# First layer of a fused two-block model: values before scores, casts moved off the recurrence, head squares taken early

## The reference, cut to what matters

```
qa, fa, ia, ga, xb, yb = split_cols(h @ even_w_in[e], EVEN_SIZES)
oa = hgrn2_mix(qa, fa, ia, ga, lb_all[l], hgrn_norm[e])      # 4 heads of 128
ob = rglru_mix(xb, yb, ...)                                   # a scan over the 256 tokens
mix = concatenate([oa, ob]) @ even_w_out[e]
# inside hgrn2_mix, per head:
scores = causal(q_dec @ (kh * exp(-bcum)).T)                  # inside a chunk of 64
o = scores @ vh + q_dec @ S_prev                              # S: state from chunk to chunk
o = o * rsqrt(mean(o * o) + EPS) * norm_gain * sigmoid(g)
```

## Time and profile before

| what | value |
|---|---|
| median of 3 runs | 1753.26 us (1750.53 to 1753.48) |
| the profiled execution: its time, its span | 1751.99 us, 1750.3 us |
| TensorE, VectorE, ScalarE, GpSimd busy | 93%, 62%, 47%, 8% |
| mean granted TensorE clock | 0.974 of full speed |
| the first layer with its last output tile | about the first 148 us of the span |

### The profile page before, as it was taken

How to read it: one execution, slowest core, us unless ns; L and a number is a source line. 1 busy time by engine, 2 the same in 40 slices (tenths; PEclk the granted TensorE clock), 3 DMA queues, 4 the chain that set the end, 5 groups by cost and what they waited for, 6 DMA issues and landing times.

```text
span 1750.3 us, 23355 instructions
## 1 busy us (share of the span) xinstructions
PE 1621.3 (93%) x9060; PEld 1347.4 (77%) x9060; DVE 1093.4 (62%) x1985; ACT 827.6 (47%) x1512; POOL 139.4 (8%) x153
## 2 busy tenths in 40 slices
PE   7977999988989999989999899999998879999998
PEld 7866888977868887867768676787777768887886
DVE  6666667775558868664475777615547655464565
ACT  5845444554656555442204454333324345455564
POOL 0100111111310203100000000000001000000000
PEclk9998999999999999999999999999999989999999
DMA  7433666644326544424401111124422213242333
GB/s 251 147 97 122 216 238 219 206 133 145 108 99 197 177 145 133 158 86 166 169 0 61 61 37 48 54 80 168 157 97 84 85 60 104 96 137 74 133 105 124
DMA packets 61885, 217.69 MB, mean 124 GB/s; under 512 B 7888, under 2 KB 8144, under 8 KB 61648
## 3 DMA queue, kind: packets, MB, share of 16 engines
q1 hardware_dynamic: 58608, 212.40, 36.2%
q10 hardware_dynamic: 3168, 3.80, 0.7%
HBM read 215.09 MB, written 1.05 MB: 123 GB/s over the span
## 4 chain that ended last, share of the span: by engine, by line
PE 64%; DVE 15%; ACT 12%; issue 6%; POOL 1%; ACTq 1%; DMA 1%; DVEq 0%; POOLq 0%
PE PS L328 18%; PE PS L330 17%; PE PS L329 17%; DVE WL L304 4%; ACT WH L293 3%; PE PS L470 2%; PE PS L2494 2%; PE PS L1936 2%; PE PS L1945 2%; PE PS L746 1%; POOL AR L1488 1%; ACT TMP L396 1%; PE PS L2525 1%; DVE AR L1437 1%; DVE X L443 1%
## 5 line engine op out<-in xcount | busy, mean ns | idle before, releaser
L304 DVE TENSOR_TENSOR WL<-RAWB,WH 128x1024 fp32r<-128x1024 f32 x346 | 429.1, 1247 | 240.0 <-ACT WH L293 236.5
L328 PE MATMUL PS<-RH,WH 128*128 128x256 f32 (+1 forms) x1560 | 504.2, 323 | 25.3 <-DVE WL L304 9.9
L329 PE MATMUL PS<-RH,WH 128*128 128x256 f32 (+1 forms) x1560 | 491.4, 315 | 0.0
L330 PE MATMUL PS<-RH,WL 128*128 128x256 f32 (+1 forms) x1560 | 491.4, 315 | 0.0
L293 ACT CAST WH<-RAWB 128x1024 fp32r<-128x1024 f32 x346 | 357.2, 1041 | 240.1 <-PE PS L330 191.7
L328 PEld LDWEIGHTS PS<-RH,WH 128*128 128x128 f32 x1560 | 299.0, 192 | 63.6 <-issue 12.0
L328 PE MATMUL PS<-WH,RH 128*128 128x512 f32 (+1 forms) x768 | 309.5, 403 | 20.7 <-DVE WL L304 12.6
L329 PEld LDWEIGHTS PS<-RH,WH 128*128 128x128 f32 x1560 | 299.5, 192 | 18.0 <-issue 0.5
L330 PEld LDWEIGHTS PS<-RH,WL 128*128 128x128 f32 x1560 | 299.0, 192 | 18.5
L329 PE MATMUL PS<-WL,RH 128*128 128x512 f32 (+1 forms) x768 | 299.4, 390 | 0.0
L330 PE MATMUL PS<-WH,RH 128*128 128x512 f32 (+1 forms) x768 | 299.4, 390 | 0.0
(11 more groups left out here) (331 smaller groups left out, 1657.9 us busy)
## 6 DMA issues: line engine op xcount, KB each, us to landing
RAWB<-ws SPq DMA_DIRECT2D x394, 512.0 KB, 3.6
TMP<-gains ACTq DMA_DIRECT2D x8, 256.0 KB, 3.1
CS<-cs SPq DMA_DIRECT2D x1, 1472.0 KB, 8.1
X<-x SPq DMA_DIRECT2D x2, 512.0 KB, 3.9
X<-ctx SPq DMA_DIRECT2D x2, 512.0 KB, 7.1
AR<-dec ACTq DMA_DIRECT2D x2, 512.0 KB, 7.1
out<-X SPq DMA_DIRECT2D x4, 256.0 KB, 2.0
AR<-rgw SPq DMA_DIRECT2D x1, 512.0 KB, 5.0
```

Of the source, the lines that this page charges most:

```text
L304: dve.e.tensor_tensor(k.WL[:, i % SPL, :], k.RAWB[:, i % RAW, :], k.WH[:, i % SPL, :].bitcast(F32), ALU.subtract).then_inc(*dve.done("wl", i))
L328: pe.e.matmul(o, wh, xh, start=first, stop=False)
L329: pe.e.matmul(o, wh, xl, start=False, stop=False)
L330: return pe.e.matmul(o, wl, xh, start=False, stop=last)
```

## The change

The first layer's order is rewritten, in all four engines:

- TensorE projects the values right behind y; step 0 of the heads follows. The list of steps is new, and the output tiles stand later among the heads' steps.
- ScalarE casts chunk 14 before the logarithms, 22 before gelu, 23 before the roots, 24 and 25 at scan blocks 0 and 1; the blocks 2 and 3 have none. All four scores are copied out after the values.
- VectorE makes the low parts 22 before the root's argument and 23, 24, 25 at blocks 0, 1, 2; the turned keys are copied after the scan.
- A head's output gets a buffer of its own (four, in the place of E3, in stead of two), and is squared right behind its copy. Its rounding is a step 4 of its own.
- GpSimd makes (G + 1) * half the norm gain for every head ahead, and multiplies it with the head's output; VectorE then has one product (with the root) where it had two operations.

```diff
-EVEN_STEPS = [("h", 0, 1), ("h", 1, 1), ("out", 0, 0), ("h", 0, 2), ("h", 2, 1), ("out", 1, 0), ("h", 0, 3), ("h", 1, 2),
-              ("h", 3, 1), ("out", 2, 0), ("h", 1, 3), ("h", 2, 2), ("out", 3, 0), ("h", 2, 3), ("h", 3, 2), ("out", 4, 0),
-              ("h", 3, 3)]
+EVEN_STEPS = [(u[0], int(u[1]), int(u[2])) for u in
+              "h01 h11 t00 h02 h21 h12 h31 t10 h03 h22 h13 h32 t20 h04 h23 h33 h14 t30 h24 t40 h34".split()]
-        self.OH = [view(13056 + 256 * i, 256) for i in range(2)]
+        self.OH = [self.E3[:, i, :] for i in range(4)]
 even_pe
+    project_tokens(k, pe, (s, "v"), "even_w_in", 8, 8, blocks(L.HH), 2, 512, ready)
     for h in range(4):
         head(h, 0)
-    project_tokens(k, pe, (s, "v"), "even_w_in", 8, 8, blocks(L.HH), 2, 512, ready)
 even_act
+    cast_to(k, act, k.ws.chunk(s, "g", 0) + 2)
     act.e.preload_act_table_set(LNEXP)
...
+    v0 = k.ws.opens(s, "v", 0)
+    cast_to(k, act, v0 + 2)
     for j in range(4):
         act_(L.YG[:, j, :], first("y", j), ACT.Gelu_apprx_tanh).then_inc(*act.done(s, "gelu", j))
-    scores(0)
-    scores(1)
+    cast_to(k, act, v0 + 3)
     for j in range(4):
         act.wait_ge(*k.DVE.at(s, "root", j))
         act_(L.R[:, j, :], L.R[:, j, :], ACT.Sqrt).then_inc(*act.done(s, "root", j))
-    scores(2)
-    scores(3)
     for j in range(4):
-        cast_to(k, act, v0 + j + 1)
+        if j < 2:
+            cast_to(k, act, v0 + j + 4)
         act.wait_ge(*k.DVE.at(s, "rgout", j))
         act_(L.Y[0][:, 4 + j, :], L.I[:, j, :], ACT.Copy).then_inc(*act.done(s, "yh", 4 + j))
...
+    for h in range(4):
+        scores(h)
...
         elif p == 2:
             act.wait_ge(*k.PE.at(s, "o", h))
-            act.wait_ge(*k.ACT.at(s, "yh", h - 2))
-            act.wait_ge(*k.DVE.at(s, "yl", h - 2))
-            act_(L.OH[h % 2], k.ps.of(s, "o", h)[:, 0:256], ACT.Copy).then_inc(*act.done(s, "o", h))
+            act_(L.OH[h], k.ps.of(s, "o", h)[:, 0:256], ACT.Copy).then_inc(*act.done(s, "o", h))
             k.ps.free(act, s, "o", h)
-        elif p == 3:
             x = k.sq.take(act, (s, h), "sq", 0)[:, 0:256]
             act.wait_ge(*k.ACT.at(s, "o", h))
-            act_(x, L.OH[h % 2], ACT.Square).then_inc(*act.done((s, h), "sq", 0))
+            act_(x, L.OH[h], ACT.Square).then_inc(*act.done((s, h), "sq", 0))
+        elif p == 3:
             rstd_act(k, act, (s, h), 256, 128, True)
+        elif p == 4:
             act.wait_ge(*k.DVE.at(s, "gated", h))
-            act_(L.Y[0][:, h, :], L.OH[h % 2], ACT.Copy).then_inc(*act.done(s, "yh", h))
+            act_(L.Y[0][:, h, :], L.OH[h], ACT.Copy).then_inc(*act.done(s, "yh", h))
 even_dve
+    ahead("g", 0)
...
+    v0 = k.ws.opens(s, "v", 0)
+    rest_to(k, dve, v0 + 2)
...
-    turned_keys(0)
-    turned_keys(1)
     for j in range(4):
-        rest_to(k, dve, v0 + j + 1)
-        if j < 2:
-            turned_keys(2 + j)
+        if j < 3:
+            rest_to(k, dve, v0 + j + 3)
...
+    for h in range(4):
+        turned_keys(h)
...
         elif p == 3:
             rstd_dve(k, dve, (s, h), 256, 128)
-            v.scalar_tensor_tensor(o, o, L.hgn[:, h:h + 1], r, ALU.mult, ALU.mult).then_inc(*dve.done())
-            v.scalar_tensor_tensor(o, L.G[:, h, :], 1.0, o, ALU.add, ALU.mult).then_inc(*dve.done(s, "gated", h))
+            dve.wait_ge(*k.POOL.at(s, "og", h))
+            v.tensor_tensor(L.OH[h], L.OH[h], k.rb.of((s, h), "r")[:, 0:256], ALU.mult).then_inc(*dve.done(s, "gated", h))
+        elif p == 4:
             dve.wait_ge(*k.ACT.at(s, "yh", h))
 even_pool
     for h in range(4):
+        pool.e.tensor_scalar(L.G[:, h, :], L.G[:, h, :], 1.0, L.hgn[:, h:h + 1], ALU.add, ALU.mult).then_inc(*pool.done())
+    for h in range(4):
         causal(h)
+    for h in range(4):
+        pool.wait_ge(*k.ACT.at((s, h), "sq", 0))
+        pool.e.tensor_tensor(L.OH[h], L.OH[h], L.G[:, h, :], ALU.mult).then_inc(*pool.done(s, "og", h))
```

More of the change, by code:

```diff
@@ L967, in even_pe @@
             plain(kind, h)
+    project_tokens(k, pe, (s, "v"), "even_w_in", 8, 8, blocks(L.HH), 2, 512, ready)
     for h in range(4):
         head(h, 0)
-    project_tokens(k, pe, (s, "v"), "even_w_in", 8, 8, blocks(L.HH), 2, 512, ready)
     for kind, n, p in EVEN_STEPS:
-        if kind == "h":
+        if kind == "t":
+            back(n)
+        elif p < 4:
             head(n, p)
-        else:
-            back(n)
     back(5, 6, 7)
@@ L1046, in even_act @@
         act_(L.R[:, j, :], L.R[:, j, :], ACT.Sqrt).then_inc(*act.done(s, "root", j))
-    scores(2)
-    scores(3)
     act.e.preload_act_table_set(LNEXP)
-    v0 = k.ws.opens(s, "v", 0)
     for j in range(4):
-        cast_to(k, act, v0 + j + 1)
+        if j < 2:
+            cast_to(k, act, v0 + j + 4)
         act.wait_ge(*k.DVE.at(s, "rgout", j))
         act_(L.Y[0][:, 4 + j, :], L.I[:, j, :], ACT.Copy).then_inc(*act.done(s, "yh", 4 + j))
-    cast_to(k, act, k.ws.chunk(s, "v", 0) + 2)
     for n in range(2):
@@ L1059, in even_act @@
         k.ps.free(act, s, "v", n)
+    for h in range(4):
+        scores(h)
+    cast_to(k, act, k.ws.chunk(s, "v", 0) + 2)
     for kind, h, p in EVEN_STEPS:
-        if kind == "out":
+        if kind == "t":
             out_ahead(k, act, s, [h], cast_to)
@@ L1242, in even_dve @@
             rstd_dve(k, dve, (s, h), 256, 128)
-            o, r = L.OH[h % 2], k.rb.of((s, h), "r")[:, 0:256]
             dve.wait_ge(*dve.last())
-            dve.wait_ge(*k.ACT.at((s, h), "sq", 0))
-            v.scalar_tensor_tensor(o, o, L.hgn[:, h:h + 1], r, ALU.mult, ALU.mult).then_inc(*dve.done())
+            dve.wait_ge(*k.POOL.at(s, "og", h))
+            v.tensor_tensor(L.OH[h], L.OH[h], k.rb.of((s, h), "r")[:, 0:256], ALU.mult).then_inc(*dve.done(s, "gated", h))
             k.rb.free(dve, (s, h), "r")
-            dve.wait_ge(*dve.last())
-            dve.wait_ge(*k.ACT.at(s, "g", h))
-            v.scalar_tensor_tensor(o, L.G[:, h, :], 1.0, o, ALU.add, ALU.mult).then_inc(*dve.done(s, "gated", h))
+        elif p == 4:
             dve.wait_ge(*k.ACT.at(s, "yh", h))
-            v.tensor_tensor(L.Y[1][:, h, :], o, L.Y[0][:, h, :].bitcast(F32), ALU.subtract).then_inc(*dve.done(s, "yl", h))
+            v.tensor_tensor(L.Y[1][:, h, :], L.OH[h], L.Y[0][:, h, :].bitcast(F32), ALU.subtract).then_inc(
+                *dve.done(s, "yl", h))
     out_ahead(k, dve, s, [5, 6, 7], rest_to)
@@ L1271, in even_pool @@
     for h in range(4):
+        pool.wait_ge(*k.ACT.at(s, "g", h))
+        pool.wait_ge(*k.DVE.at(s, "kh", 0))
+        pool.e.tensor_scalar(L.G[:, h, :], L.G[:, h, :], 1.0, L.hgn[:, h:h + 1], ALU.add, ALU.mult).then_inc(*pool.done())
+    for h in range(4):
         causal(h)
+    pool.wait_ge(*pool.last())
+    for h in range(4):
+        pool.wait_ge(*k.ACT.at((s, h), "sq", 0))
+        pool.e.tensor_tensor(L.OH[h], L.OH[h], L.G[:, h, :], ALU.mult).then_inc(*pool.done(s, "og", h))
     seam_pool(k, pool, seams(k)["ffn0"])
```

## The result

| | median | runs | |
|---|---|---|---|
| before | 1752.85 us | 4 | 1750.53 to 1753.48 |
| changed | 1737.89 us | 4 | 1735.16 to 1739.35 |

The ratio is 0.9915, 95% interval [0.9898, 0.9932]: 15 us less, by the interval 12 to 18. The profiled execution took 1737.17 us, with a span of 1735.1. A later comparison (five runs against nine) gave 0.9940 [0.9926, 0.9953], 10.5 us less. The two intervals meet between 12 and 13 us less, and the layer itself gives 12.

A forecast was written before the change was run, and what follows sets the result against it. TensorE's waits for VectorE and ScalarE, and the lower clock after longer ones, were taken to bound the first layer; its end moving from 148.1 to 138.1 us gave 10.0 us less, 1742.0 us, range 1737 to 1749.

The forecast's parts named there:

- rival A: Wait before out5: a 3.0 us wait costs no clock, so 11.9 us less, or 13.1; chance 0.20 (over 12 less).
- Before 79 us: nothing.: Up to the end of y: moving chunk 14's cast counts 0; at most 1.5 us gained or 1 us lost.
- Values end 90.3: TensorE's four value chunks follow y without a pause and end at 90.3 us, before 98.70.
- Scan.: Scan blocks wait for a cast only once; block 3 ends 95.8 us, out0 starts 101.0, 4.4 us sooner.
- out0's clock.: After TensorE's near idleness from 92 to 101 us, all of out0 runs at the lower clock, 5.1 us.
- VectorE's tail.: From the first sum of squares, at 113.6 us, VectorE carries the rest; low part 29 done at 127.3, 31 at 130.3.
- GpSimd's share: Two GpSimd products beside VectorE's chain delay it by 2 x 0.54 = 1.1 us, bounds 0 and 4.3.
- The wait before out5: TensorE, done with out4 at 124.3 us, waits 3.0 us for out5; twelve matmuls then run at 1.2 GHz.
- rival D: All 96 wide output matmuls run at 1.2 GHz, costing 14.8 us more: 1756.8 us, slower; chance 0.03.
- Sum: First layer's last output matmuls end at 138.1 us, before 148.1: 10.0 us less, 1742.0 us.
- Rival B: All eight GpSimd operations delay VectorE and one removed wait returns at 1.7 us: 5 us less, 1747 us; chance 0.22.
- C: Next layer's weights are the bound, so an earlier end only lengthens its first matmul's wait: 1752 us; chance 0.05.

The follow-up runs named there:

- the gate on VectorE: Changed kernel with the gate's two operations back on VectorE and none on GpSimd; ratio to the kernel before 0.9947, layer 75.14 us.
- more GpSimd: Changed kernel with two more unread GpSimd products behind each head's product; layer 72.46 us against 71.06 changed, one run.
- the heads' half alone: Kernel before with the new head steps, four output buffers, early squares and GpSimd's products, values and scores as before; ratio 0.9948, layer 73.93 us.
- filling both pauses: Changed kernel with value, score and turned-key copies made earlier and unread matmuls in both TensorE pauses ahead of out0; ratio to the kernel before 0.9921, layer 66.00 us.

## Why the prediction was right, and where its size was off

The forecast was 10.0 us less, 1742.0 us; it came out at 1737.9, inside the range. The forecast's own case (9 to 12 us less) did not come in this comparison; rival A (over 12, chance 0.20) did, and the later comparison, with 10.5 us less, would fall into the forecast's. That 1737.9 lies even below rival A's own sum of 11.9 us less is owed to 2.9 us outside the layer that no term of the prediction holds. By its own steps (the prediction's times are those of the trace before, in which the last gate projection starts 0.72 us later than in the changed one; 0.72 is added here to the measured times):

- *Before 79 us: nothing.* Right: without the edit on chunk 14, out0 starts as late.
- *Values end 90.3.* Right, 0.4 us early: 89.21 + 0.72 = 89.9. Nothing waits for a weight.
- *Scan.* Block 3 was to end at 95.8, value copies at 97.1, scores at 100.9, out0 to start at 101.0: measured 95.8, 97.1, 100.9 and 101.25. The circle of cast and copy was left in one block only, as said. That out0 then hangs on ScalarE's queue was tested by taking the copies forward: 3.1 us. (The profile names VectorE's last state, L1235, as what released out0, after 0.61 us; that state stands behind the scores.)
- *out0's clock.* 5.1 us taken, 5.25 measured.
- *VectorE's tail.* Start 113.6, low part 29 done at 127.3: measured 114.4 and 127.1: it starts 0.8 us later, and its work takes 1.0 us less than summed (a head's five operations took 2.25 us, for 2.4). GpSimd's share was put at 1.1 us: 0.83 us in the trace, and a run that adds operations adds delay. The rule of the Trainium skill ("SBUF — State Buffer", section "Who interferes with whom") on the ports that both share agrees with both: every VectorE operation that was held up had two operands in SBUF, and L709, which reads PSUM, kept its 0.41 us beside GpSimd's products.
- *The wait before out5.* **The step that was off.** I let out4 end at 124.3; it ended at 124.73 + 0.72 = 125.45. Two sums and two states took 3.9 us for 3.5, the four small groups before out2 3.0 for 2.9, out0 ended 0.4 late, the output chunks took the rest. Low part 29 came 0.2 us early. So the wait was 1.74 us by the profile in place of 3.0, and the term "twelve matmuls at 1.2 GHz", 2.2 us, measured 0: that was rival A. That a 3 us wait here costs the clock is borne out: where the gate on VectorE makes this wait 3.00 us, the clock falls and costs 2.5 us; at 2.76 us (more GpSimd) it costs 1.4; at 1.74 or 1.75 us it costs nothing, in seven traces. The mechanism was right, the pause was taken 1.3 us too long. The small groups of TensorE make 0.5 us of that: from start to start the two sums ahead of out1 took 1.30 and 1.31 us, where the row gave 1.15. Why they took longer is not shown; the granted clock was 0.89 in the first and 1.00 in the second.
- *What the rows said of the clock.* Two readings were off. Behind the wait of 4.06 us stood 24 matmuls, not 36, so twelve of 24 ran at the lower clock (rival D counts 36). And the wait of 1.80 us before the first value chunk, which the prediction lists but does not weigh, did bring the lower clock: its first seven matmuls ran at 1.2 GHz (granted clock 0.50 from 83.98 to 87.10 us), as did those behind a wait of 1.81 us in the heads' half alone (0.54 over 3.7 us). So the length of a wait alone does not decide, and that 1.74 us would cost nothing did not follow from the rows. Nor does the length set the price: 4.05 us cost 1.5 and 3.00 us cost 2.5.
- *Sum.* The layer gave 12.1 us: the 10.0 of the sum and the 2.2 of this term, with the smaller misses cancelling. The remaining 2.9 us of the measured 15 lie outside the layer. The clock of the first turns and of the seam accounts for 1.9 of the 3.1 us by which the spans differ beyond the layer (5.36 and 5.44 us for 32 turning matmuls, 6.09 and 6.62 before); the other 1.2 us in the later layers lies within their scatter, and the second comparison did not repeat it. That is argued from the traces, and not from a run that fixes the clock.
- *Rival B* (5 us less): GpSimd's delays were as priced, no removed wait came back. *C*: the next layer took the whole gain along; its first matmul waits 1.48 us in both kernels. *D*: from the end of out0 to out5 the mean clock was 0.99, and 1.00 from there to the seam.

What stays open: whether filling both pauses shows in the medians, what decides whether a wait of some 1.8 us costs the clock, and how much of the first comparison's 15 us belongs to its chip.

## What to carry to other kernels

When several engines feed one another in program order, the worth of a reordering is found by writing the queues out once with the row's durations: here this gave the start of out0 within 0.3 us and VectorE's last low part within 0.2. What pays is the distance between a result and its reader (7.6 of 12.1 us came from moving the output tiles so that a head's rounding stands well behind its sum of squares: 5.0 from shorter waits, 2.6 from the clock that the shorter last wait kept), more than the single operation saved. Small groups that recur are worth pricing with some room: a sum of 1.15 us in the rows took 1.3 at its new place. Where a pause lies between those of the traces that kept the clock and those that lost it, carry both cases: here 1.0 us more of it (1.74 to 2.76) cost 1.4 more, and 1.3 us (to 3.00) 2.5.

## What the runs showed of the hardware

- After a pause of 1.74 or 1.75 us before out5 TensorE's clock stayed at 2.4 GHz, after 2.76 us and 3.00 us it was lower for part of the last 36 matmuls (mean 0.83 and 0.74), for 1.4 and 2.5 us. Pauses of 4.06, 4.05 and 3.96 us before the last 24 cost 2.4, 1.5 and 2.6 us, and one of 1.80 us, behind 3.1 us of the heads' short step 0, cost the first seven matmuls the full clock.
- In one trace each: with 40 matmuls in the first pause and then 4.9 us in which TensorE was busy for 3.0, the clock was 1.00 in both and fell inside the next chunk, 0.61 on average; with both pauses filled that chunk ran at 1.00.
- Where a GpSimd product held up a VectorE operation with two SBUF operands, it cost 0.3 to 0.42 us. GpSimd is held up as well: 1.01 us in place of 0.73 behind an operation of 0.43 us, and in the changed kernel 1.23 to 1.29 us in place of 0.48 for its operations on G (L1273) that began inside a low part.
